# Second block of a two-block float32 network: split operands in its output projections and attention scores, and the position bias moved to the panels' queue

## What is computed

```python
def second_block(x, c, ctx, ...):
    for layer in range(DEPTH):                       # DEPTH = 2
        h = modulated_norm(x, ...); h_ctx = modulated_norm(x_ctx, ...)
        p = jnp.matmul(h, w_in[layer]); p_ctx = jnp.matmul(h_ctx, w_in[layer])
        # layer 0 (even): global attention + context attention, and a long convolution (hyena)
        # layer 1 (odd): windowed attention and neighbourhood attention
        y, y_ctx = even_mixer(...) or odd_mixer(...)
        x = x + gate[:, None] * jnp.matmul(y, w_out[layer])
        if need_ctx:                                 # layer 0 only
            x_ctx = x_ctx + c_gate * jnp.matmul(y_ctx, w_out[layer])
    return x
# in each attention: s = (q . k) * 64 ** -0.5 (+ mask or position bias); p = softmax(s); o = p . v
```

## Time and profile before

| | |
|---|---|
| median of 3 runs | 2621.21 us (2615.28 to 2623.82) |
| the profiled execution | 2622.54 us, of which the span is 2620.7 us |
| PE busy | 2455.6 us (94%) |
| DVE busy | 1735.7 us (66%) |
| ACT busy | 1317.0 us (50%) |
| chain that ended last | PE 81%, DVE 10%, ACT 4% |
| mean granted PE clock | 0.968 of full speed |

### The profile page before, as it was taken

The page is one execution under the profiler, slowest core; times in us unless marked ns, Lnnn a source line. Parts: engine busy times, 40 slices in busy tenths (PEclk is TensorE's granted clock), DMA queues, the critical chain, the costliest instruction groups (busy, mean ns, idle before and its releaser), DMA issues.

```text
span 2620.7 us, 34792 instructions
## 1 busy us (share of the span) xinstructions
PE 2455.6 (94%) x13668; PEld 2024.2 (77%) x13681; DVE 1735.7 (66%) x1665; ACT 1317.0 (50%) x1303; POOL 31.7 (1%) x25
## 2 busy tenths in 40 slices
PE   6898999988986999999999999999979998988998
PEld 6898999988985888888888888887448734538967
DVE  5764544467545888888888888886366434616684
ACT  6454434354724767676767777775232201403353
POOL 0100000001000000000000000000000000000000
PEclk9999999989987999999999999999989999999989
DMA  6234455433433989898989999998602222042200
GB/s 238 94 132 145 159 179 180 173 113 113 142 132 115 372 332 375 331 374 331 374 331 366 341 352 352 355 351 334 232 33 81 97 97 96 7 91 81 97 1 17
DMA packets 81633, 531.50 MB, mean 203 GB/s; under 512 B 16919, under 2 KB 17080, under 8 KB 17336
## 3 DMA queue, kind: packets, MB, share of 16 engines
q1 hardware_dynamic: 71856, 523.11, 53.3%
q10 hardware_dynamic: 9672, 6.88, 1.4%
HBM read 528.90 MB, written 1.05 MB: 202 GB/s over the span
## 4 chain that ended last, share of the span: by engine, by line
PE 81%; DVE 10%; ACT 4%; issue 2%; ACTq 1%; DMA 1%; SPq 0%; DVEq 0%
PE ps L386 79%; ACT arena L1141 1%; PE ps L1079 1%; ACTq L1632 1%; ACT B_high L1141 1%; PE ps L804 1%; DVE ring_low L1752 1%; DVE h_parts L2267 1%; DVE arena L1859 1%; DVE arena L1866 1%; ACT L1141 1%; DVE arena L1876 1%; ACT P_high L1141 0%; DVE arena L1851 0%; DMA ring<-panels 0%
## 5 line engine op out<-in xcount | busy, mean ns | idle before, releaser
L2084 DVE TENSOR_TENSOR ring_low<-ring,M_high 128x2048 fp32r<-128x2048 f32 x336 | 760.8, 2290 | 124.8 <-ACT M_high L1141 113.1
L1141 ACT ACTIVATE M_high<-ring 128x2048 fp32r<-128x2048 f32 x336 | 631.2, 1908 | 3.1 <-DMA ring<-panels 3.0
L386 PE MATMUL ps<-M_high,xe_parts 128*128 128x512 f32 x1792 | 600.4, 397 | 2.4 <-DVE xe_parts L2095 2.4
L386 PEld LDWEIGHTS ps<-M_high,xe_parts 128*128 128x128 f32 x1792 | 337.2, 188 | 70.2 <-DVE xe_parts L2095 2.6
L386 PE MATMUL ps<-ring_low,xe_parts 128*128 128x512 f32 x896 | 350.3, 391 | 0.0
L1141 ACT ACTIVATE arena<-ps 128x256 f32<-128x256 f32 (+3 forms) x237 | 115.2, 486 | 299.8 <-PE ps L386 268.0
L386 PE MATMUL ps<-h_parts,B_high 128*128 128x256 f32 x1024 | 193.5, 291 | 21.0 <-DVE ring_low L1752 13.4
L386 PE MATMUL ps<-h_parts,ring_low 128*128 128x256 f32 x704 | 204.3, 290 | 0.0
L386 PEld LDWEIGHTS ps<-ring_low,xe_parts 128*128 128x128 f32 x896 | 169.1, 189 | 32.4
L386 PEld LDWEIGHTS ps<-h_parts,B_high 128*128 128x128 f32 x1024 | 164.9, 198 | 22.8 <-DVE ring_low L1752 14.1
L386 PE MATMUL ps<-M_high,hid_high 128*128 128x512 f32 x448 | 175.9, 393 | 2.1 <-DVE hid_low L2090 2.1
(11 more groups left out here) (249 smaller groups left out, 4401.1 us busy)
## 6 DMA issues: line engine op xcount, KB each, us to landing
ring<-panels SPq DMA_DIRECT2D x496, 1024.0 KB, 4.8
arena<-rpb ACTq DMA_DIRECT2D x32, 64.0 KB, 6.4
cst<-consts SPq DMA_DIRECT2D x1, 1760.5 KB, 8.8
xT<-x SPq DMA_DIRECT2D x1, 1024.0 KB, 4.8
cT<-ctx ACTq DMA_DIRECT2D x1, 1024.0 KB, 7.8
arena<-dft ACTq DMA_DIRECT2D x1, 1024.0 KB
y<-xT ACTq DMA_DIRECT2D x1, 1024.0 KB, 3.9
proj<-w ACTq DMA_DIRECT2D x1, 512.0 KB
```

The costliest lines, as they stand in the source:

```text
L386: return nc.tensor.matmul(o, w, m, start=start, stop=stop, skip_group_check=skip)
L1141: return nc.scalar.activation(o, i, fn, **kw)
L2084: V.tensor_tensor(wide_low(q, 0, PW), ring[:, (q % RING) * PW:(q % RING + 1) * PW], moe_high(q, 0, PW).bitcast(F32), ALU.subtract).then_in ...
```

## The change

1. **Output projections.** `out2` uses `mm3` in both layers. ACT copies each of the 8 chunks of y and each of the 4 panels (`out_chunk_high`, `out_panel_high`), DVE subtracts (`out_chunk_low`, `out_panel_low`). The first chunk and panel 0 are split inside `attend`, after unit 22 (`Y_EARLY`), and in layer 1 panel 1 after unit 30.
2. **Scores.** Query and key are split and stacked: a tile of 128 partitions has a head's 64 rows twice. In layer 0 and for the window units the query tile has high over low and there is a key tile of high twice and one of low twice; for the neighbour units the key tile has high over low and the query tiles are high twice and low twice. Two float32r products of depth 128 replace one plain product of depth 64. The keys and the first queries of layer 0 are split in `hyena`, those of the window units in `project2(1)`; the other two query chunks of layer 0 at the end of units 8 and 16, the eight neighbour heads at the end of units 2, 5, 8, 11, 19, 21, 23 and 25 (`SPLITS`).
3. **Position bias.** Its 32 transfers leave ACT's queue for SP's, four behind each of eight panel loads of `project2(1)`.

```diff
+        Y_FIRST = ((4, 5, 6, 7, 0, 1, 2, 3), (0, 1, 2, 3, 4, 5, 6, 7))
+        Y_high = (over("Y_high_0", at_arena, 0, KD * 512), over("Y_high_1", at_proj, 0, KD * S))
+        O_high = ((over("O_high_0", at_proj, (C_HU + 8) * 512, PW), over("O_high_1", at_arena, 4096, PW)),
+                  (over("O_high_2", at_proj, C_G * 512, PW), over("O_high_3", at_arena, 0, PW)))
...
+        Y_EARLY = 22
...
+        Stacks = (over("Stacks_0", at_proj, C_HU * 512, 4096), over("Stacks_1", at_hT, 0, 4096))
+        Window_keys = over("Window_keys", at_cT, 0, 2048)
+        Window_queries = over("Window_queries", at_proj, 0, 10 * 512)
...
+        def query_tile(layer, c, half):
+            if layer:
+                at = (c + 6 * half) * 512 + S
+                return Window_queries[:, at:at + S]
+            at = 2048 + (c % 2) * 1024 + half * 512
+            return Stacks[0][:, at:at + 512]
+        def neighbour_tiles(h):
+            at = (h % 4) * 1024
+            return Stacks[1][:, at:at + S], Stacks[1][:, at + S:at + 512], Stacks[1][:, at + 512:at + 1024]
...
+        SPLITS = ([(8, ("q", 2)), (16, ("q", 3))],
+                  [(2, ("n", 0)), (5, ("n", 1)), (8, ("n", 2)), (11, ("n", 3)),
+                   (19, ("n", 4)), (21, ("n", 5)), (23, ("n", 6)), (25, ("n", 7))])
...
-                    q=proj[r, (C_Q + c) * 512 + stream * S + qt * P:][:, 0:P],
-                    k=proj[r, C_K * 512 + stream * S:(C_K + 1) * 512],
+                    scores=lambda a, b: [
+                        (query_tile(layer, c, half)[:, stream * S + qt * P:][:, 0:P],
+                         key_tile(layer, half, low)[:, stream * S + a:stream * S + b]) for low in range(2)],
...
-                    q=proj[r, (C_NQ + c) * 512 + qt * P:][:, 0:P], k=proj[r, (C_NK + c) * 512:(C_NK + c + 1) * 512],
+                    scores=lambda a, b: [(neighbour_tiles(h)[low][:, qt * P:(qt + 1) * P], neighbour_tiles(h)[2][:, a:b])
+                                         for low in range(2)],
...
+            biases = [(h, r) for h in range(8) for r in range(4)]
+            for p in range(looped * RING, PANELS):
                 sp.wait_ge(DONE, p - RING + 1)
                 load(p, p % RING)
+                if p - RING + 1 >= last_mixer:
+                    for h, r in biases[:4]:
+                        src = bass.AP(rpb_in.tensor, h * 465 + (7 - r) * 31 + 15 - 63, [[1, 64], [31, 4], [1, 64]])
+                        dst = arena[(r % 2) * 64:(r % 2) * 64 + 64, (h * 2 + r // 2) * S:(h * 2 + r // 2 + 1) * S]
+                        sp.dma_start(dst.rearrange("p (a b) -> p a b", a=4), src) \
+                          .then_inc(sem("position_bias_landed"), 16)
+                    biases = biases[4:]
...
+                        pe.wait_ge(sem("scores_split"), splits_for(layer, i))
+                        def score(o, a, b):
+                            (q0, k0), (q1, k1) = u["scores"](a, b)
+                            mm(o, q0, k0, True, False)
+                            return mm(o, q1, k1, False, True)
                         if u["kind"] == "plain":
-                            last = mm(bank(i % 2)[:, 0:u["keys"]], u["q"], u["k"], True, True)
+                            last = score(bank(i % 2)[:, 0:u["keys"]], 0, u["keys"])
                         else:
-                            mm(bank(i % 2)[:, 0:S], u["q"], u["k"][:, 0:S], True, True)
-                            last = mm(bank(6 + i % 2)[:, 0:S], u["q"], u["k"][:, S:512], True, True)
+                            score(bank(i % 2)[:, 0:S], 0, S)
+                            last = score(bank(6 + i % 2)[:, 0:S], S, 512)
...
                 for j in range(OUTP):
                     if layer == 0 and j == 3:
                         pe.wait_ge(sem("ada_taken"), 2)
-                    q = take()
-                    for m in range(2):
-                        for k in range(KD):
-                            last = mm(bank(2 * j + m)[:, 0:n], slot(q, k * 256 + m * P, k * 256 + (m + 1) * P),
-                                      y3[:, k, 0:n], k == 0, k == KD - 1)
+                    pe.wait_ge(sem("out_panel_split"), nth(pe, "out_panel_split"))
+                    q = at[0]
...
+                    at[0] += 1
+                    high = O_high[layer][j % 2]
+                    for k, m in ([(k, m) for k in Y_FIRST[layer] for m in range(2)] if j == 0 else
+                                 [(k, m) for m in range(2) for k in Y_FIRST[layer]]):
+                        if j == 0 and m == 0:
+                            pe.wait_ge(sem("out_chunk_split"), nth(pe, "out_chunk_split"))
+                        a, b = k * 256 + m * P, k * 256 + (m + 1) * P
+                        last = mm3(bank(2 * j + m)[:, 0:n], (high[:, a:b], wide_low(q, a, b)), chunk(k),
+                                   k == Y_FIRST[layer][0], k == Y_FIRST[layer][-1])
...
+                    if layer and p == 6:
+                        act.wait_ge(sem("window_turned"), 1)
+                        keys_high(1)
+                    elif layer and 7 <= p < 11:
+                        query_high(1, p - 7)
...
+                keys_high(0)
+                query_high(0, 0)
+                query_high(0, 1)
...
+            def neighbour_high(h):
+                high, _, key = neighbour_tiles(h)
+                r, c = half_rows(h % 2), h // 2
+                for to in range(2):
+                    f(high[half_rows(to), :], proj[r, (C_NQ + c) * 512:(C_NQ + c) * 512 + S], ACT.Copy)
+                f(key[r, :], proj[r, (C_NK + c) * 512:(C_NK + c + 1) * 512], ACT.Copy) \
+                    .then_inc(sem("scores_high"), 1)
...
+                    for at, (kind, c) in SPLITS[layer]:
+                        if at == i and kind == "q":
+                            act.wait_ge(sem("scores_ready"), 8 * (c - 1))
+                            query_high(0, c)
+                        elif at == i:
+                            if c >= 4:
+                                act.wait_ge(sem("scores_ready"), n + 16 + 2 * (c - 3))
+                            neighbour_high(c)
+                    if i == Y_EARLY:
+                        if layer:
+                            act.wait_ge(sem("o_gated"), n + 16)
+                        out_chunk_high(layer, Y_FIRST[layer][0])
+                        out_panel_high(layer, 0)
+                    if i == n - 2 and layer:
+                        act.wait_ge(sem("scores_ready"), 2 * n - 6)
+                        out_panel_high(layer, 1)
...
+            def out_panel_high(layer, j):
+                q = panel[0] + j
+                act.wait_ge(LANDED[q % RING], 16 * (q // RING + 1))
+                if j >= 2:
+                    act.wait_ge(DONE, q - 1)
+                f(O_high[layer][j % 2], ring[:, (q % RING) * PW:(q % RING + 1) * PW], ACT.Copy) \
+                    .then_inc(sem("out_panel_high"), 1)
+            def out2(layer):
+                act.wait_ge(sem("y2_ready"), nth(act, "y2_ready"))
+                for k in Y_FIRST[layer][1:]:
+                    out_chunk_high(layer, k)
+                if layer:
+                    out_panel_high(layer, 2)
+                    out_panel_high(layer, 3)
+                    return
+                act.wait_ge(sem("ada_taken"), 2)
+                out_panel_high(layer, 1)
+                narrow_part(panel[0] + OUTP, 0)
+                narrow_part(panel[0] + OUTP, 1)
+                out_panel_high(layer, 2)
+                square_both(0)
+                out_panel_high(layer, 3)
+                for j in range(1, 4):
+                    square_both(j)
...
-                    narrow_part(panel[0], 1)
-
-                    act.wait_ge(sem("y2_ready"), nth(act, "y2_ready"))
-                    for h in range(8):
-                        for r in range(4):
-                            src = bass.AP(rpb_in.tensor, h * 465 + (7 - r) * 31 + 15 - 63, [[1, 64], [31, 4], [1, 64]])
-                            dst = arena[(r % 2) * 64:(r % 2) * 64 + 64, (h * 2 + r // 2) * S:(h * 2 + r // 2 + 1) * S]
-                            act.dma_start(dst.rearrange("p (a b) -> p a b", a=4), src) \
-                               .then_inc(sem("position_bias_landed"), 16)
-                    for j in range(4):
-                        square_both(j)
...
+                out2(layer)
...
+                    if layer and p == 5:
+                        announce("window_turned")
+                    elif layer and p == 7:
+                        keys_low(1)
+                    elif layer and 8 <= p < 12:
+                        query_low(1, p - 8)
...
+            def neighbour_low(h):
+                high, low, key = neighbour_tiles(h)
+                r, c = half_rows(h % 2), h // 2
+                dve.wait_ge(sem("scores_high"), nth(dve, "scores_high"))
+                for to in range(2):
+                    V.tensor_tensor(low[half_rows(to), :], proj[r, (C_NQ + c) * 512:(C_NQ + c) * 512 + S],
```

(68 more changed lines are left out.)

44 lines of the change are left out of this document (43 added, 1 removed).

## The result

| | before | after |
|---|---|---|
| median, 13 runs each | 2617.44 us (2608.41 to 2623.82) | 2625.77 us (2622.67 to 2629.03) |
| the profiled execution | 2622.54 us, span 2620.7 | 2625.77 us, span 2624.0 |
| mean granted PE clock | 0.968 | 0.965 |

The ratio is 1.0034, with a 95% interval from 1.0023 to 1.0045: the change makes the kernel 8.3 us slower. I had forecast 2620, no measurable change, so the result is inside the range of the prediction and outside its likeliest case. That it lies inside at all owes something to the base: the forecast was 1.2 us under a median of three runs of 2621.2, and over 13 runs that kernel's median is 2617.4.

The account below looks back on a forecast made before the run. PE was taken to lead everywhere, with DVE within 0.25 us per unit of bounding attend(1). Terms -20.7 - 4.7 + 19.8 + 2 = -3.6, plus 2 for the clock, gave about 2620 us, range 2612 to 2629.

Parts of the forecast that it names:

- out2(0): Layer 0 output projection: four split panels save 12.0 us, and the wait and slow stretch go too; -20.7 us.
- out2(1): Layer 1 output projection: four plain panels take 27.88 us, split ones 23.0; -4.7 us.
- attend(1), splits: Layer 1 attention: eight neighbour heads cost 19.6 us, chunk and panel 0 4.3, panel 1 3.9; sum 27.8.
- attend(1), gain: Layer 1 attention: split scores remove DVE's 4.0 us of waiting, about 1 in window units, 3 at the start; -8.
- attend(0), splits: Layer 0 attention: two query chunks at 2.9 us each, chunk and panel 0 at 5.0, some slack; 10 us.
- attend(0), gain: Layer 0 attention: split scores save PE products, at most 9.8 us, taken as 8.
- clock in attend(0): Layer 0 attention: no clock term of its own; the stage's net was +2 us, from +1 to +11.
- norm, project2(1): Norm and layer 1 projection: splits hidden by PE's panels, taken at nothing; 6.1 us if uncovered.
- the allowance: Whole kernel: 2 us added because PE idles about 2.5 us at each split and some stretch may run at 1.2 GHz.
- rival 2: In attend(1) the clock stays at 1.2 GHz, 17 units lose 1.5 us each, some 25; 2645 us; chance 0.22.
- Rival 1: In both attentions the splits are hidden and cost nothing; -41 us, 2580 us; chance 0.1 for the whole.
- rival 3: In project2(1) bias transfers delay panel loads and it waits, some 10 us; 2630 us; chance 0.05.

Follow-up runs that it names:

- e1: The kernel before with only the 32 bias transfers moved from ACT's queue to SP's; 2611.24 us, ratio 0.9985.
- e8: The changed kernel with output projections plain again in both layers, without their splits; 2624.78 us, ratio 1.0023.
- e5: The changed kernel with 24 extra unused PE products behind each of the three splits of attend(0); 2619.13 us, ratio 1.0004.
- e4: The changed kernel with 24 extra unused PE products at each of nine splits of attend(1); 2625.62 us, ratio 1.0032.
- e2: The changed kernel with all scores plain again, split output projections and bias on SP kept; 2623.45 us, ratio 1.0025.
- e3: The changed kernel with only the neighbour heads' scores plain again, so their eight splits inside attend(1) are gone; 2610.00 us, ratio 0.9977.
- e7: The changed kernel with all splits that stood inside the attend units made by GpSimd alone; 2598.79 us, ratio 0.9921.
- e9: The changed kernel with all attend splits on GpSimd, output panels copied and subtracted in 8 pieces of 256 columns; 2581.01 us, ratio 0.9853.
- e10: The changed kernel with each neighbour head's copies spread one per unit on ACT, each subtraction a unit later on DVE; 2619.01 us, ratio 1.0003.
- e6: The changed kernel with plain scores and 12 extra unused PE products behind each output panel split inside attend; 2611.69 us, ratio 0.9985.

## Why the prediction was wrong, term by term

| term | predicted | measured | from |
|---|---|---|---|
| out2(0) | -20.7 | -18.6 | stages; -8.9 of it the bias (e1), -9.7 the split (e8) |
| out2(1) | -4.7 | -4.7 | stages |
| attend(1), splits | +27.8 | +31.3 | periods, the 0.6 of two slow units with them |
| attend(1), gain | -8 | -6.6 | the stage's +24.7 less the splits; -4.2 against e1 |
| attend(0), splits | +10 | +9.5 | 2.74 + 2.73 + 4.6, less 0.6 in the unit behind the last |
| attend(0), gain | -8 | -9.1 | +5.9 less splits and clock |
| clock in attend(0) | in the +2 | +5.5 | periods; e5 takes it away |
| norm, project2(1) | 0 | -0.2 | stages |

The predicted column sums to -3.6, with the allowance -1.6; the stages measured give +7.1 and the medians +8.3. These stages are of one execution of each kernel; for `attend(0)` the sum of +5.9 lies in the range of +1 to +11 that I had given.

**The step that failed is the allowance, "To it I add 2 for the clock".** It stood for the whole kernel, and no row gave its size. The clock cost 5.5 in `attend(0)` alone, 1.5 in the first panel of `out2(0)`, which began at 1.2 GHz, and 0.6 in two slow units of `attend(1)`: 7.6 instead of 2, which is 5.6 of the 8.7 between my sum of -1.6 and the +7.1. I had taken the clock seriously as rival 2, but for the wrong stage: I looked at `attend(1)`, and for `attend(0)` took the mean clock of 0.96 as a defence. A mean from before, when PE waited often and briefly, says nothing of waits of 3 us.

Rival 2's own reasoning was half right. In `attend(1)` the clock did fall: 0.86 over the stage, and 0.50 from 2557 to 2565, far behind the first 20 us, which I had named as this rival's sign. The Trainium skill ("TensorE: Matmul & The Clock Gate", What's actually happening) says that the slow state is the default and activity releases it; that the clock fell where PE's work became less agrees with that. The sign came without the price of 25: e4 shows that it cost about 1 us there. A unit's work on PE at the low clock is about 4.3 us (1.12 + 1.97 + 1.22 at 2560). That fits into the 5 of a unit with a split, and slow units mostly fell on those. Where they did not, as in e8, they cost 5. With plain scores PE has more to do per unit, and against e1 e2 paid 9.6 and 12.5 for splits whose own cost is at most 4.6 and 7.7.

**The second miss is a size.** A neighbour split was taken at 2.45 and is 2.8: ACT's read of the accumulator behind the exponential (2548.17 instead of 2548.07), and 0.1 from the last copy to DVE's start. Eight times 0.35 is 2.8 of the 3.5. The trace of the kernel before had that read already, behind the exponential of 2546.87, and I passed over it:

```profile
2547.49 0.19 ACT L1141 ACTIVATION_READ_ACCUMULATOR arena<-arena,stat 128x1 f32 x1
```

The mechanism, subtractions queued between the gating and the next unit with DVE's slack gone, was right, and e3, e7, e9 and e10 bear it out.

**Smaller ones.** `out2(0)`: the layout of ACT's and DVE's queues held, with nothing late; 1.5 of the missing 2.1 is its slow start. The gain of split scores is larger in `attend(0)` and smaller in `attend(1)` than I said, where DVE's wait per unit was the most that could be gained (0.5 of its 4.0 us is left). Rival 1 (hidden splits) did not happen, nor rival 3: no SP transfer was waited for. The rate of split products was that of the row, 0.227, in `out2(0)` too, not the 131 ns that the Trainium skill ("TensorE: Matmul & The Clock Gate", Back-to-back issue gap) gives.

Still open: why the clock stayed low in the first units of `attend(0)` in e6, why the start of `out2(0)` is slow in some kernels and not in others, what decides the scatter ahead of `attend(0)`, and why the kernel before scatters over 15 us and the changed one over 6; no run was made for these.

## What to carry to other kernels

Before adding work to an engine between two steps of a pipeline, find that engine's idle time per step. Where it was a quarter of a microsecond, as here, every operation put there was paid in full, together with the wait for whatever feeds it, and splitting operands that two units use did not earn that back. Count the idle time that the new work makes on TensorE as well: each long wait can be paid a second time at 1.2 GHz, and it is paid where TensorE is near to being the bound, which the mean clock of the old profile does not tell. Work without a deadline belongs on an idle engine, in short instructions.

## What the runs showed of the hardware

DVE's scaling from SBUF to SBUF waits for the GpSimd instruction under way: 0.49 became 4.78 beside a 128x2048 subtraction of 4.50, and at most 1.02 beside shorter ones (e9). DVE's maxima did not wait (0.42 and 0.69 beside GpSimd as without it). The Trainium skill ("SBUF — State Buffer", Who interferes with whom) says that GpSimd and DVE in its two-port modes, which a `tensor_scalar` can enter and a `tensor_reduce` cannot, share a port pair that whoever issues first holds for its whole instruction; these rows agree, and e9 shows that shorter instructions are the remedy. GpSimd's speeds were those of ACT for a copy (128x2048 in 1.90) and half of DVE's for a subtraction (4.50 against 2.29).
